# A transformer block's second mixer, restaged: its panels, its compression, its attention units and its recurrence in a new order

## The reference, cut to what matters

```
proj = hn @ w_in                         # q, six key/value blocks, gates; then hq, hf, hi, hg (4 heads of 128 each)
kc, vc = compress(k_c), compress(v_c)    # blocks of 32 tokens, stride 16: gelu(flat @ w1) @ w2
p_c = softmax(q @ kc - slope * distance); o_cmp = p_c @ vc
o_sel, o_win = attention of 8 heads of 64 over the 512 tokens, with a slope per head, two branches
nsa = g0 * o_cmp + g1 * o_sel + g2 * o_win
f = lower + (1 - lower) * sigmoid(hf);  k = (1 - lower) * (1 - sigmoid(hf));  q = silu(hq)
S_t = diag(f_t) S_{t-1} + k_t^T hi_t;   o_t = q_t S_t          # the recurrence, 4 heads, state 128 x 128
y = rms_norm(o) * silu(hg)
h = h + concat(nsa, y) @ w_out
```

## Time and profile before

| | us |
|---|---|
| three runs, median (lowest to highest) | 3244.49 (3244.05 to 3244.86) |
| the profiled execution, its own time | 3247.84 |
| its span | 3246.1 |
| mean granted clock of PE, share of full speed | 0.948 |
| PE busy over the span | 2988.5 (92%) |
| second mixer, from its first load to the next layer's first load | 514.0 |

### The profile page before, as it was taken

The page is one execution under the profiler, slowest core; times in us unless marked ns, Lnnn a source line. Parts: engine busy times, 40 slices in busy tenths (PEclk is TensorE's granted clock), DMA queues, the critical chain, the costliest instruction groups (busy, mean ns, idle before and its releaser), DMA issues. The chain is left out here.

```text
span 3246.1 us, 41178 instructions
## 1 busy us (share of the span) xinstructions
PE 2988.5 (92%) x14412; PEld 2532.8 (78%) x14412; DVE 1780.9 (55%) x3727; ACT 1025.8 (32%) x1471; POOL 840.7 (26%) x511
## 2 busy tenths in 40 slices
PE   7789879999989999989999998999886998889997
PEld 6657667888868888879999996888765776768885
DVE  5564444956667774048888866442331545454423
ACT  3222331333334444223333333332211333132321
POOL 0022200444423333467666610000032212100000
PEclk9879989999989999989999999999986998899998
DMA  4012232444344455479999963333230212033231
GB/s 142 19 62 95 104 106 70 138 135 133 124 145 168 170 184 197 143 264 382 354 354 352 354 233 98 100 95 98 84 132 33 75 41 98 17 99 103 91 100 63
DMA packets 179309, 466.73 MB, mean 144 GB/s; under 512 B 21729, under 2 KB 71521, under 8 KB 177634
## 3 DMA queue, kind: packets, MB, share of 16 engines
q1 hardware_dynamic: 155490, 372.56, 34.1%
q0 software_dynamic: 22528, 67.19, 5.4%
q10 hardware_dynamic: 1152, 25.17, 1.9%
HBM read 395.44 MB, written 69.21 MB: 143 GB/s over the span
## 5 line engine op out<-in xcount | busy, mean ns | idle before, releaser
L54 PE MATMUL cb_y<-cb_g_hi,cb_b_hi 128*128 128x384 f32 x1024 | 343.1, 335 | 15.1 <-DVE cb_g_lo L1779 15.1
L55 PE MATMUL cb_y<-cb_g_lo,cb_b_hi 128*128 128x384 f32 x1024 | 342.8, 335 | 0.0
L56 PE MATMUL cb_y<-cb_g_hi,cb_b_lo 128*128 128x384 f32 x1024 | 342.8, 335 | 0.0
L186 DVE TENSOR_TENSOR ffn_lo<-ffn_raw,ffn_hi 128x1024 fp32r<-128x1024 f32 x132 | 161.4, 1226 | 273.4 <-ACT ffn_hi L182 273.4
L54 PE MATMUL ffn_bank<-x_hi,ffn_hi 128*128 128x512 f32 x704 | 277.4, 394 | 25.5 <-DVE x_lo L122 23.1
L55 PE MATMUL ffn_bank<-x_lo,ffn_hi 128*128 128x512 f32 x704 | 275.2, 391 | 0.0
L56 PE MATMUL ffn_bank<-x_hi,ffn_lo 128*128 128x512 f32 x704 | 275.0, 391 | 0.0
L491 POOL TENSOR_TENSOR bs_lo<-bs_raw,bs_hi 128x1024 fp32r<-128x1024 f32 x72 | 174.6, 2426 | 320.5 <-ACT bs_hi L468 320.5
L54 PE MATMUL bs_ps<-x_hi,bs_hi 128*128 128x512 f32 x576 | 229.5, 398 | 14.9 <-POOL bs_lo L491 14.9
L182 ACT CAST ffn_hi<-ffn_raw 128x1024 fp32r<-128x1024 f32 x132 | 137.9, 1048 | 301.2 <-PE ffn_bank L56 260.0
L1755 ACT CAST cb_b_hi<-cb_b_raw 128x1024 fp32r<-128x1024 f32 x128 | 134.6, 1051 | 304.7 <-PE cb_y L56 290.0
(11 more groups left out here) (459 smaller groups left out, 6703.6 us busy)
## 6 DMA issues: line engine op xcount, KB each, us to landing
cb_b_raw<-in_peer_v SPq DMA_DIRECT2D x128, 512.0 KB, 6.8
ffn_raw<-in_gu SPq DMA_DIRECT2D x88, 512.0 KB, 3.5
bs_raw<-in_peer_u SPq DMA_DIRECT2D x72, 512.0 KB, 3.5
rs_raw<-in_peer_u SPq DMA_DIRECT2D x56, 512.0 KB, 3.5
routing<-br_out ACTq DMA_DIRECT2D x8, 3072.0 KB, 9.1
cb_route<-routing SPq DMA_DIRECT2D x32, 768.0 KB, 8.3
cb_unit<-hidden SPq DMA_DIRECT2D x128, 192.0 KB, 6.1
ffn_raw<-in_down SPq DMA_DIRECT2D x44, 512.0 KB, 3.5
```

What stands on the lines that cost most here:

```text
L54: pe.matmul(out, w_high, x_high, start=first, stop=False)
L55: pe.matmul(out, w_high, x_low, start=False, stop=False)
L56: return pe.matmul(out, w_low, x_high, start=False, stop=last)
L186: dve.tensor_tensor(lo[:, k % R, :], raw[:, k % R, :], hi[:, k % R, :].bitcast(F32), ALU.subtract).then_inc(split, 1)
```

## The change

The second mixer becomes three stages.

1. `project_and_compress`: the norm, the 11 panels and 8 of the 16 (`HG_FIRST`: hf and hq), three weight slots in place of four. Between the panels stands the compression: transpositions after panels 6 and 7, `w1` in eight parts of 1 MB (two after each of panels 7 to 10), hidden layer after 11, `kcT` and `vc` after 12, one tile's scores after each of 13 to 16, and its values two panels later. The forget gates, keys and queries of the recurrence are prepared in the last panels. The results stay in SBUF. The attention bias is one table (`far`) for all heads, since queries and scale take up the slope.
2. `attend_and_recur`: the 64 units with, between them, the other 8 panels (two weight slots, one bank, two steps per unit from unit 4, then 1.5 to unit 41) and the steps of the recurrence, at most one kind per unit: same-token products in units 0 to 3, one half level in each of 4 to 17, and so on. Transposed probabilities have one bank in place of two. POOL multiplies the keys of a level (DVE did) and makes the low parts. The attended tokens are transposed at units 52, 54, 56 and at the end.
3. `project_onto` with the whole output projection, 8 panels.

The store to `hg_proj` and its reload are gone. The diff, cut to its core:

```diff
+    R = 3
+    n_nsa, n = len(NSA_ORDER), len(NSA_ORDER) + len(HG_FIRST)
+    EARLY = 6
+    TURN_AT = {6: (0, 1), 7: (2, 3)}
+    PART_AT = 7
+    GELU_AT = PART_AT + N_PARTS // 2 - 1
+    HTURN_AT, KC_AT, SCORE_AT = GELU_AT + 1, GELU_AT + 2, GELU_AT + 3
...
+                for k in range(n):
+                    panel(k)
+                    if k == 1:
+                        norm.tensor(pe)
+                    for t in TURN_AT.get(k, ()):
+                        turn(t)
+                    if 0 <= k - PART_AT < N_PARTS // 2:
+                        hidden_part(2 * (k - PART_AT))
+                        hidden_part(2 * (k - PART_AT) + 1)
+                    if k == HTURN_AT:
+                        turn_hidden()
+                    if k == KC_AT:
+                        keys_and_values()
+                    t = k - SCORE_AT
+                    if 0 <= t < TILES:
+                        score(t)
+                    if 0 <= t - 2 < TILES:
+                        result(t - 2)
+                    if 0 <= t - 1 < TILES:
+                        turn_weights(t - 1)
...
+                norm.vector_add(dve)
+                low_part(3)
+                norm.vector_inverse(dve)
+                low_part(4)
+                take(0)
...
+                for k in range(EARLY, n):
+                    behind(k - 1)
+                    take(k)
+                    if k + R < n:
+                        low_part(k + R)
+                behind(n - 1)
...
-        self.t_ps = [c.ps(f"{name}_t{i}", [P, SEQ]) for i in range(2)]
+        self.t_ps = [c.ps(f"{name}_t{i}", [P, SEQ]) for i in range(banks)]
...
+            if between is not None:
+                between(i)
             if 1 <= i <= n:
                 j = i - 1
                 pe.wait_ge(self.exped, j + 1)
-                if j >= 2:
-                    pe.wait_ge(self.copied, j - 1)
+                if j >= self.banks:
+                    pe.wait_ge(self.copied, j - self.banks + 1)
...
+    SAME_AT, LEVEL_AT, V_AT = 0, 4, 23
+    K_AT = (28, 29, 30)
+    WRITE_AT = (32, 34, 37)
+    TILE_AT = (31, 36, 39, 41)
+    MEAN_AT = 43
+    Y_AT = 47
+    O_AT = (52, 54, 56)
...
+    def steps_by(i):
+
+        n = min(2 * max(i - FROM, 0), N_LAST // 2 * KC)
+        return min(n + 3 * max(i - FROM - N_LAST // 4 * KC, 0) // 2, N_LAST * KC)
...
+            def double_keys(m, e):
+                pool.wait_ge(S["scored"], 2 * m + e + 1)
...
+                pool.tensor_tensor(early, early, both[:, :, 1:2].broadcast_to(early.shape), ALU.mult
+                                   ).then_inc(S["keys_doubled"], 1)
...
+            for i in range(n_units):
+                if i in cast_at:
+                    low_part(cast_at.index(i))
+                if level_of(i):
+                    double_keys(*level_of(i))
...
+            def level(m, e):
+                if m:
+                    pe.wait_ge(S["doubled"], 2 * (m - 1) + e + 1)
+                    pe.wait_ge(S["keys_doubled"], 2 * (m - 1) + e + 1)
+                    pe.wait_ge(S["masked"], 2 * (m - 1) + e + 1)
...
+                if i == MEAN_AT:
+                    act.wait_ge(S["taken"], N_LAST)
+                    act.activation(flat(gate), flat(gate), ACT.Silu).then_inc(S["gate"], 1)
+                    act.wait_ge(S["mean"], 1)
+                    act.activation(root[:], root[:], ACT.Sqrt).then_inc(S["root"], 1)
...
+            def beside(i):
+                if 0 <= i - 1 - SAME_AT < 4:
+                    if i - 1 == SAME_AT:
+                        dve.wait_ge(S["zeros"], 1)
+                        dve.wait_ge(S["masks"], 2 * LEVELS + 1)
+                    place_same(i - 1 - SAME_AT)
+                if level_of(i - 1):
+                    double(*level_of(i - 1))
+                    place(*level_of(i - 1))
+                if i in last_of:
+                    take(last_of.index(i))
...
-        hgrn_stage(nc, d["hg_proj"], o_tok, ident, d["lower_bound"], d["out_norm"], d["w_out"], x_hi, x_lo, hT)
+            att = Attention(c, "att2", [unit(t, h, branch) for t in range(TILES) for branch in (1, 2)
+                                        for h in range(NSA_HEADS)], ident, banks=1)
+            attend_and_recur(nc, att, c, d["w_hg"], proj, hg, f, qp, rstd, ident, d["out_norm"], o_tok, x_hi, x_lo)
+
+    project_onto(nc, "wo2", x_hi, x_lo, d["w_out"], hT)
```

More of the change, by code:

```diff
@@ L1952, in compress_and_attend @@
         o_ps = c.ps("cp_ops", [P, SEQ])
[L1953 to L1955 removed]
+        norm = NormStage(c, "p2", hT, d["mix_norm"], o_ps, o_tok[:, 0:2], None, o_tok[:, 2:4], rstd[:])
         S = {x: c.sem(f"cp_{x}") for x in (
[L1957 to L1958 removed]
@@ L1959, in compress_and_attend @@
-        n_small = 3
+            "high", "split", "product", "taken", "plain_high", "plain_split",
+            "w", "hturned", "hidden", "cleared", "const", "scaling", "biases", "turned", "copied", "gates", "gated", "blocks",
+            "part_used", "hid", "gelu", "kc", "kcopied", "scored", "seq", "shifted", "exped", "weights", "pturned", "pcopied",
+            "out", "stored", "lb", "lb_shift", "lb_exp", "sig", "nsig", "silu", "f", "key", "query")}
+        landed = [c.sem(f"p_landed{i}") for i in range(R)]
@@ new lines, in keys_and_values @@
+                def keys_and_values():
+                    pe.wait_ge(S["w"], 16 * 3)
+                    pe.wait_ge(S["hidden"], 1)
+                    for g in range(NSA_GROUPS):
+                        for i in range(2):
+                            at = NSA_HD * (1 - g)
+                            last = pe.matmul(o_ps[:, 0:NB], w2k[:, i, at:at + P], hidden[:, 0, i, g, :],
+                                             start=g == 0 and i == 0, stop=g == 1 and i == 1)
+                    for g in range(NSA_GROUPS):
+                        for i in range(2):
+                            last = pe.matmul(o_ps[0:NB, P + g * NSA_HD:P + (g + 1) * NSA_HD], hidden[:, 1, i, g, :],
+                                             w2v[:, i, :], start=i == 0, stop=i == 1)
+                    last.then_inc(S["kc"], 1)
@@ L2158, in _, with store, forget @@
                                       ).then_inc(S["weights"], 1)
+                def store(t):
                     dve.wait_ge(S["out"], t + 1)
                     dve.tensor_copy(o_tok[:, t, :], o_ps[:]).then_inc(S["stored"], 1)
-    clear_semaphores(nc, S.values())
+                def forget(e):
+                    dve.wait_ge(S["sig"], e + 1)
+                    for h in range(PAIR[e].start, PAIR[e].stop):
+                        last = dve.tensor_scalar(f[:, h, :], f[:, h, :], free[:, h:h + 1], lb[:, h:h + 1], ALU.mult, ALU.add)
+                    then(last)
+                    dve.tensor_scalar(flat(f[:, PAIR[e]]), flat(f[:, PAIR[e]]), F_FLOOR, None, ALU.max
+                                      ).then_inc(S["f"], 1)
+                    dve.wait_ge(S["nsig"], e + 1)
+                    for h in range(PAIR[e].start, PAIR[e].stop):
+                        last = dve.tensor_scalar(z[:, h, :], z[:, h, :], free[:, h:h + 1], None, ALU.mult)
+                    last.then_inc(S["key"], 1)
@@ new lines, in _ @@
+                low_part(7)
+                take(4)
+                fill_blocks(1)
+                dve.wait_ge(S["scaling"], NSA_HEADS)
+                take(5)
+                low_part(8)
+                dve.wait_ge(S["lb_exp"], 1)
+                then(dve.reciprocal(lb[:], lb_e[:]))
+                then(dve.tensor_tensor(lb_e[:], lb_e[:], lb[:], ALU.mult))
+                then(dve.tensor_tensor(lb[:], lb_e[:], lb_e[:], ALU.subtract))
+                then(dve.tensor_scalar(free[:], lb[:], -1.0, 1.0, ALU.mult, ALU.add))
@@ new lines, in unit @@
+        def unit(t, h, branch):
+            part = slice(h // 4 * NSA_HD, (h // 4 + 1) * NSA_HD)
+            w, at = (t + 1) * P, (TILES - 1 - t) * P
+            keys, values = ((KSEL, vsel), (KWIN, vwin))[branch - 1]
+            return dict(q=proj[part, NQ0 + h % 4, t * P:(t + 1) * P], k=proj[part, keys, :w], width=w,
+                        bias=far[:, at:at + w], v=lambda b: values[:, b, part], dv=NSA_HD, add=True,
+                        gate=gates[:, t, 3 * h + branch:3 * h + branch + 1], scale=float(NSA_HD) ** -0.5 * slope_of(h),
+                        out=o_tok[:, t, h * NSA_HD:(h + 1) * NSA_HD])
```

1145 lines of the change are left out of this document (577 added, 568 removed).

## The result

The changed kernel takes 3223.78 us (median of 7 runs, 3206.04 to 3228.3) beside 3244.86 for the kernel before on the same chip: ratio 0.9925, 95% interval 0.9902 to 0.9948. It is faster by 21 us where 62 were forecast, and lies outside the range. The kernel before keeps within 4 us; the runs of the changed one spread over 22, which is itself a reading. The profiled execution is one of the long ones, 3228.3 (span 3226.6).

A forecast was written before the change was run, and what follows sets the result against it. TensorE (PE) was taken as the bound, needing 392 of 514 us; stages of 173.5 + 224.1 + 54.1 = 451.7 against 514.0, 62.3 less, gave a 3182.2 us median, range 3164 to 3212.

The forecast's parts named there:

- 48 to 63: Stage two's last units, without panels: about 2.48 us each at PE's own pace, 44.6 with transposes and crowded VectorE units.
- units 42 to 47: Stage two: 18.2 us, including 4.3 for ScalarE's stop for Silu, root and table loads, and 1.8 for norms.
- I am wrong if stage two lasts over 250: Stated sign of failure for stage two, which was forecast at 224.1 us.
- Stage one: Projection and compression: panels and compression at full clock, plus start, tail and stalls; 173.5 us to the next stage.
- Head of stage two: Units 0 to 3: VectorE waits for POOL's masks, PE stops, then runs at clock 0.50; 15 us.
- Levels: Units 4 to 17, two panel steps and half a level each: units of 4.0 us, key doublings on POOL 1.6.
- Stage three: Output projection, eight panels, same code as the first mixer's; 54.1 us.
- A: Whole kernel PE-bound, as the terms sum: 3182 us; chance 0.55.
- B: VectorE and POOL block each other, 41.6 us on VectorE, over half reaching PE: +24, 3206 us; chance 0.22.
- C: Less delay stays: mask stall shrinks from 15 to 9, collisions and ScalarE's stop vanish; 3168 us; chance 0.15.
- D: Levels become a chain through POOL's key doublings; gain gone at 8.4 us per unit, slower beyond; chance 0.03.
- E: Panels don't hide: late casts stall panels in stages one and two, +48, 3230 us; chance 0.05.

The follow-up runs named there:

- busy_stop: Changed kernel plus 24 useless 512-column matmuls on TensorE where it would wait during ScalarE's stop; 3183.4 us.
- spread: tanh with VectorE's mask wait moved to the first level, the last four panels spread to unit 49 and result turns set later; 3173.0 us.
- keys_on_dve: busy_stop with the fourteen key doublings moved from POOL back to VectorE; 3183.9 us.
- burst_small: Changed kernel plus 144 additional 128-column matmuls in units 47 and 48, after ScalarE's stop; 3242.1 us.
- tanh: Changed kernel with the gate's Silu computed by tanh and the root by Newton's rule, so no table loads at unit 43; 3211.8 us.
- no_loads: Changed kernel with the gate's Silu and the norm's root replaced by plain copies, output not the same; 3202.9 us.
- burst_later: Changed kernel plus 48 additional 512-column matmuls in units 47 and 48, after ScalarE's stop; 3201.2 us.
- masks_late: busy_stop with VectorE's wait for POOL's masks moved from unit 1 to the first level; 3180.0 us.

## Why the prediction was wrong

**The step that failed** is "48 to 63: no panel is left to fill ... just PE's own 2.48", together with the line before it for units 42 to 47. Both took PE's times at full clock as given. The order of the work was right (ScalarE's stop, 4.3 by the sum, is 5.2 in the trace), and the units do take 2.48 where the clock is 1.00. But the sum asked what a stop costs while it lasts, and not at which clock TensorE goes on after it. busy_stop is the prediction without that error: its stages are 177.3, 220.9 and 53.3 us, 451.5 in all, against 173.5 + 224.1 + 54.1 = 451.7. Its stages miss by +3.8, -3.2 and -0.8, so that the sums agree to 0.2 us is luck; that each stage is within 4 is not. Almost the same work with the clock lost takes 263.1 in stage two, 42.2 more.

**The rows had a warning.** The compression of before was granted 0.67 over 98.9 us, and 0.50 in its part of narrow matmuls, the tiles of the earlier trace rows. I halved the price of that part because it would stand between panels. The same reading said what the last 22 units, which have none, might be exposed to, though it couldn't settle it: these tiles also had waits of 2.81 and 1.14 us between their matmuls. None of the five rivals held it: all five spoke of waits. The one test of mine that pointed to it was "I am wrong if stage two lasts over 250", and it came true with 263.1.

**By the steps.** *Stage one:* 5.4 us over. The stretch 2480 to 2490 of the changed kernel ran at 0.66 with PE busy for 10.00 of 10, from the narrow matmuls of the compression on: 3.4 us of it, and no hole lay before the fall. spread's trace has 1.00 there, and its stage one is 175.6. The rest is the tail, 9.1 for 6.7. (10 us at 0.66 do the work of 6.6.) *Head of stage two:* 15.3 against 15. *Levels:* key doublings 1.51 and 1.24 (1.6 taken), units 4.07 (4.0). Stage two up to 2657.6 is 15.3 + 133.7 = 149.0 against 148.1. *Stage three:* 54.4 against 54.1. *A* was therefore right in its mechanism for all but the last 22 units and a short stretch of stage one. *B:* its mechanism is there, its price isn't. VectorE's operations do last longer beside POOL's in the levels (timeline of DVE and POOL, changed kernel):

```profile
2549.20 2.38 POOL L2483 TENSOR_TENSOR hp_lo<-hp_raw,hp_hi 128x1024 fp32r<-128x1024 f32 x1 [2.42 <-ACT hp_hi L2642]
2550.69 1.42 DVE L2698 TENSOR_TENSOR hg_qp<-hg_qp,hg_total 128x512 f32<-128x512 f32 x1
2551.53 1.60 POOL L2478 TENSOR_TENSOR hg_all<-hg_all,hg_total 128x512 f32<-128x512 f32 x1
2552.04 1.23 DVE L2699 TENSOR_TENSOR hg_total<-hg_total 128x128 f32<-128x128 f32 x1
```

The two multiplications take 0.69 and 0.28 where POOL is idle. Over stage two such excess is some 11 us on VectorE, an estimate from the durations in this trace, where B gave 41.6; and TensorE, busy for 132.82 of 133.70 us, felt almost none of it. keys_on_dve shows nothing to gain from giving POOL's work back. *C:* its time of 3168 is reached by no run; spread, without the stop and the mask wait, comes nearest with 3171.6 to 3182.6. *D:* the key chain is far from its 8.4 per level. *E:* no wait for a split in the trace.

**What stays open.** What ends the full clock in the last units is only known as far as this: wide matmuls near them keep it, and without these it is lost in most runs. Whether it is the columns of the matmuls or the share of weight loads wasn't separated; burst_small changed both at once. Why tanh lost the clock in all six runs, and no_loads with holes as large in two of four, isn't settled either. The place of the holes hardly tells them apart: tanh's begin 7.6 and 8.6 us behind the last panel step, those of no_loads 7.6 and 10.1.

## What to carry to other kernels

Before a stage is priced at full clock, ask what holds the clock there once the wide matmuls are gone. A filler spread towards the end of a stage can be worth more than the same filler used up early (spread's 3173 against tanh's 3212, of which the later mask wait may be 3 to 6 and the rest comes from spreading the panels and setting the turns later, together); and a stop of ScalarE belongs where wide matmuls follow it. If runs of one kernel spread more than those of its neighbour, compare their granted clocks before their waits.

## What the runs showed of the hardware

- TensorE busy for 85.89 of 85.90 us stayed at the lower of its two levels throughout, and twice 72 matmuls of 128 columns in a row, 15.62 us each, didn't raise it in the traced run of burst_small, while in burst_later it was up 5 us after the first of 24 with 512 columns. The Trainium skill (Perfetto Trace Analysis, section Matmul Optimizations) says that the engine scales its power with its use, so that matmuls should run back to back in batches. The wide matmuls of these traces agree; the narrow ones, though back to back, do not.
- A table load takes 1.28 us, and the activation behind it starts at once (2665.75 and 2667.04). Tanh, after exp, loads none.
- VectorE's product of two 128x1 columns took 2.02 us beside a low part on POOL, and 0.16 when POOL was idle (masks_late, timeline of DVE and POOL):

```profile
2517.12 4.66 POOL L2483 TENSOR_TENSOR hp_lo<-hp_raw,hp_hi 128x1024 fp32r<-128x1024 f32 x2
2519.77 2.02 DVE L549 TENSOR_TENSOR att_inverse<-att_inverse,n_gates 128x1 f32<-128x1 f32 x1
2521.83 0.28 DVE L555 SCALAR_TENSOR_TENSOR n_otok<-att_o,att_inverse,n_otok 128x64 f32<-128x64 f32 x1
```

  It ends as the low part does. This agrees with the exclusive lock of the Trainium skill that the prediction cites (SBUF — State Buffer, section SBUF: two separate sides). TensorE was busy for 12.00 of the 12 us from 2510 to 2522, so it cost nothing here.
